# Reordering the projections and low-rank products at the head of an RWKV-7 time-mix stage

## The chip, the cores and the metric

The kernel is one launch on one core of a Trainium2 chip (trn2). The metric is the device time in microseconds of that core, as a median over runs. TensorE does the matrix products (PE, with its weight loads as PEld), VectorE is DVE, ScalarE is ACT, GpSimd is POOL, and SyncE (SP) issues the loads of the weights.

## The reference, cut to what matters

The program is a stack of blocks over 256 tokens of width 1024: feed-forward, a first mixer, feed-forward, a "fox" mixer, feed-forward, the RWKV-7 time mix, feed-forward. The change touches only the head of the time mix:

```python
xx = _token_shift(h) - h
xr, xw, xk, xv, xa, xg = [h + xx * mu[i] for i in range(6)]
r = (xr @ w_r).astype(f32)
k = (xk @ w_k).astype(f32)
v = (xv @ w_v).astype(f32)
w = -jax.nn.softplus(-(w0 + jnp.tanh(xw @ w1) @ w2).astype(f32)) - 0.5
a = jax.nn.sigmoid((a0 + (xa @ a1) @ a2).astype(f32))
g = jax.nn.sigmoid(xg @ g1) @ g2
...
kk = heads(k * k_k.astype(f32))
kk = kk / jnp.maximum(jnp.sqrt(jnp.sum(kk * kk, axis=-1, keepdims=True)), 1e-12)
k = k * (1.0 + (a - 1.0) * k_a.astype(f32))
decay = jnp.exp(-jnp.exp(w))
```

The recurrence over time is then computed in four chunks of 64 tokens with products of scaled r, k, kk and a; for that the running sum of log decays within each chunk, and exponentials of it, are needed.

## The kernel before

**Weights.** All weights come as one stream of chunks of 1 MB (128 partitions x 2048 fp32), loaded by SP in the order of the plan into three raw buffers. RWKV_ORDER is that plan for this stage: two low-rank chunks (L0, L1), then the four k chunks RW(4) to RW(7), the four r chunks RW(0) to RW(3), RW(8), the third low-rank chunk L2, RW(9) to RW(11) (v), and the output weights. The chunks of this stage ahead of L2 are "plain": TensorE reads them in fp32 from the raw buffer, so SP may load chunk c only when chunk c-3 has been used.

**Inputs.** The inputs of the six uses (k, w, a, g, r, v) are mixed by DVE: `mix_variant(v)` writes eight tiles of 128x256 into one of two buffers, variant_x[v % 2]; VARIANTS gives the order, 1 (w), 4 (a), 5 (g), 2 (k), 0 (r), 3 (v). From the third on it waits until the use two before has read its buffer (`variant_used`). The tiles of the first variant come out mixed with the subtraction for the token shift, so at half the pace.

**TensorE.** In `rwkv_tensor` three `first` groups (products with w1, a1, g1) go ahead, then `second` products (w2, a2) in four groups b, where groups 2 and 3 wait for ACT's sigmoids of groups 0 and 1 (rw_sig) since they share four PSUM banks. Then `project` runs the four k chunks, the four r chunks and the four v chunks, each 16 products into bank 6 or 7 in turn, and each waits until the chunk two before it has been read out of its bank (bank_read). Between the k chunks stand `square_sums(b)`, one product each, that sum the squares of kk per head.

**ACT.** In `rwkv_scalar` it takes tanh, copies and sigmoids of the low-rank products, then copies each k chunk into kx, squares kk, and takes the roots of the sums, `root(b)`. It then copies the four r chunks into rr. Before each copy stands this wait, since rr until then holds (a-1)*k_a, which DVE needs for k:

```python
projected(eng, name)
eng.wait_ge(s("rw_kx"), 4)
read(nc.scalar.activation(rr[:, 2 * j:2 * j + 2, :], bank2(proj_bank(name)), ACT.Copy), name)
```

Three exponentials of the decay sums (rw_exp 1 to 3) stand before, and two after, the copies: the first after the first k chunk, the others after the four r copies.

**DVE.** In `rwkv_vector` the order is: variants 0 to 4, the running sums (`tensor_tensor_scan`, eight) and their subtraction from sw (rw_before 1), (a-1)*k_a into rr (eight), then for each k chunk kk = kx*k_k (two) and kx = (rr+1)*kx (one, rw_kx). `unit_kk(b)` (maximum, reciprocal, product, each waited for by DVE itself) divides kk by its length; the first stands after the third k chunk, the other three after variant 5. Then aa*kk, kk*sw (rw_before 2), rk = r*r_k*k (eight, after all four r chunks are read), and three products with the exponentials, after which the chunked recurrence begins.

Of the kernel before, what the change touches and what calls it, by code (L numbers as in the profile page):

```python
# [20 lines left out]
P = 128  # L21
# [26 lines left out]
def stream_plan(stages):  # L48
# [18 lines left out]
RWKV_ORDER = [("lora", 0, 0), ("lora", 0, 1)] + [("rw", 0, j) for j in (4, 5, 6, 7, 0, 1, 2, 3, 8)] + \  # L67
    [("lora", 0, 2)] + [("rw", 0, j) for j in (9, 10, 11)] + [("rw_o", 0, j) for j in range(4)]
# [118 lines left out]
def build(nc, stream, consts, vectors, x_in, rows, kept_x, out):  # L187
# [15 lines left out]
    with ctx:  # L203
# [2019 lines left out]
        VARIANTS = (1, 4, 5, 2, 0, 3)  # L2223
        FIRST_OF = {3: 4, 4: 0, 5: 8}
# [14 lines left out]
        def variant_used(eng, v):  # L2239

            if v < 3:
                eng.wait_ge(s("rw_first"), v + 1)
            else:
                eng.wait_ge(chunk_used, USE[CH[RW(FIRST_OF[v] + 3)]] + 1)

# [11 lines left out]
        def rwkv_scalar(eng, highs, st):  # L2257
# [4 lines left out]
            for b in range(4):  # L2262
                eng.wait_ge(S["turned"], 4 * n + b + 1)
                for k in (2 * b, 2 * b + 1):
                    nc.scalar.activation(ht[:, k, 1:257], psum[:, b, (k % 2) * 256:(k % 2) * 256 + 256], ACT.Copy,
                                         scale=V_AT(NORMS[n], k)).then_inc(S["h_high"], 1)
            eng.wait_ge(s("rw_first"), 2)
# [16 lines left out]
            def root(b):  # L2284

                eng.wait_ge(s("rw_sums"), b + 1)
                nc.scalar.activation(roots[:, 2 * b:2 * b + 2, :], bank2(b), ACT.Sqrt).then_inc(s("rw_root"), 1)


            for j in range(4):  # L2290
                name = RW(4 + j)
                highs.upto(CH[name] + 2)
                projected(eng, name)
                read(nc.scalar.activation(kx[:, 2 * j:2 * j + 2, :], bank2(proj_bank(name)), ACT.Copy), name)
                highs.upto(CH[name] + 3)
                if j == 0:
                    eng.wait_ge(s("rw_before"), 1)
                    nc.scalar.activation(sw, sw, ACT.Exp, scale=-DECAY).then_inc(s("rw_exp"), 1)
                eng.wait_ge(s("rw_kk"), 2 * j + 2)
                nc.scalar.activation(roots[:, 2 * j:2 * j + 2, :], kk[:, 2 * j:2 * j + 2, :], ACT.Square).then_inc(s("rw_sq"), 1)  # L2300
                if j >= 2:
                    root(j - 2)

            for j in range(4):
# [127 lines left out]
        def rwkv_vector(eng, st):  # L2432
# [27 lines left out]
            for v in range(1, 4):  # L2460
                mix_variant(v)
            eng.wait_ge(S["rw_lw"], 6)
            nc.vector.tensor_tensor(gm_lo, lw[:, 1, :], gm_hi.bitcast(F32), ALU.subtract).then_inc(s("rw_lwlo"), 1)
            nc.vector.tensor_tensor(gt_lo, lw[:, 2, :], gt_hi.bitcast(F32), ALU.subtract).then_inc(S["rw_lwlo"], 1)
            mix_variant(4)

            eng.wait_ge(s("rw_sig"), 16)
            for k in range(8):
                ins = nc.vector.tensor_tensor_scan(sums[:, k, :], const("restart", TOK), sw[:, k, :], 0.0, ALU.mult, ALU.add)
            steps(ins)  # L2470
            nc.vector.tensor_tensor(sw, sums, sw, ALU.subtract).then_inc(s("rw_before"), 1)

            for k in range(8):
# [797 lines left out]
```

## Time and profile before

| | |
|---|---|
| Median of 3 runs | 1256.83 us (1256.41 to 1257.21) |
| The profiled execution | 1255.95 us |
| Its span, first to last instruction | 1254.2 us |
| PE busy | 1231.6 us, 98% |
| DVE busy | 531.8 us, 42% |
| ACT busy | 611.1 us, 49% |
| POOL busy | 766.4 us, 61% |
| The head of the time mix, first product to the end of the last r chunk | 831.58 to 912.99 us |
| The four v chunks | 912.99 to 944.28 us |

The span is counted from the first instruction to the last; what lies around it makes the execution 1.75 us longer. The profiled execution is 0.88 us below the median. A product in plain fp32 shows as two records of TensorE in the trace, so a chunk of 16 products is 32 records. The duration of a record includes the time through the array, in which the next one already runs: the pace is read from start to start.

### The profile page before, as it was taken

How to read it: one execution, taken by the hardware profiler on the slowest of the kernel's cores; microseconds unless marked ns; L12 is line 12 of the kernel's file. 1: busy time of each engine (PE TensorE's matmuls, PEld its weight loads, DVE VectorE, ACT ScalarE, POOL GpSimd, SP SyncE). 2: the span in 40 equal slices, each digit the busy share in tenths (PEclk: the TensorE clock that was granted, in tenths of full speed). 3: DMA queues.
4: the chain of work that ended last, by engine and by line, in shares of the span. 5: the costliest groups of instructions: out<-in, count | busy, mean ns of one | idle time of the engine just before them, and what ended most of it. 6: DMA issues, size and time to landing. Idle time of an engine off the chain costs nothing.

```text
span 1254.2 us, 22959 instructions
## 1 busy us (share of the span) xinstructions
PE 1231.6 (98%) x9568; PEld 1078.5 (86%) x9568; DVE 531.8 (42%) x818; ACT 611.1 (49%) x795; POOL 766.4 (61%) x194
## 2 busy tenths in 40 slices
PE   8999999999999999999999999999998999999998
PEld 7888887888988888899998888867887998888887
DVE  4233234745343233342533222375868645332333
ACT  7455444445464444584655445444232455544442
POOL 3988870262378888675478888800034324788885
PEclk9999999999999999999999999999999999999999
DMA  7655554244345555644245555513442013555552
GB/s 294 218 179 192 201 182 140 93 169 147 123 164 203 177 194 201 209 154 166 68 168 202 201 181 189 199 71 135 149 169 83 4 38 104 187 202 184 197 194 74
DMA packets 30587, 200.79 MB, mean 160 GB/s; under 512 B 3376, under 2 KB 5296, under 8 KB 6832
## 3 DMA queue, kind: packets, MB, share of 16 engines
q1 hardware_dynamic: 27776, 195.43, 44.3%
q10 hardware_dynamic: 2736, 4.26, 1.0%
q8 instruction: 59, 0.97, 0.3%
q14 instruction: 16, 0.13, 0.0%
HBM read 197.58 MB, written 2.10 MB: 159 GB/s over the span
## 4 chain that ended last, share of the span: by engine, by line
PE 91%; DVE 4%; ACT 2%; issue 1%; POOL 1%; DMA 1%; SPq 0%; POOLq 0%; DVEq 0%
PE psum L340 25%; PE psum L342 13%; PE psum L331 10%; PE psum L333 10%; PE psum L332 10%; PE psum L973 8%; PE psum L986 3%; POOL wlo L3167 1%; PE psum L2818 1%; PE psum L2723 1%; PE psum L2834 1%; PE psum L328 1%; PE psum L586 1%; PE psum L330 1%; PE psum L329 1%
## 5 line engine op out<-in xcount | busy, mean ns | idle before, releaser
L3167 POOL TENSOR_TENSOR wlo<-raw,whi 128x2048 fp32r<-128x2048 f32 x158 | 726.9, 4606 | 377.9 <-ACT whi L301 360.5
L340 PE MATMUL psum<-f_both,whi 128*128 128x512 f32 x1408 | 492.1, 393 | 1.4 <-DVE wlo L686 1.4
L301 ACT ACTIVATE whi<-raw 128x2048 fp32r<-128x2048 f32 x157 | 300.6, 1915 | 234.2 <-PE psum L342 169.4
L342 PE MATMUL psum<-f_both,wlo 128*128 128x256 f32 x1408 | 394.6, 280 | 0.0
L340 PEld LDWEIGHTS psum<-f_both,whi 128*128 128x128 f32 x1408 | 264.4, 188 | 60.1 <-DVE wlo L686 2.0
L342 PEld LDWEIGHTS psum<-f_both,wlo 128*128 128x128 f32 x1408 | 264.8, 188 | 1.5
L331 PE MATMUL psum<-whi,ahi 128*128 128x512 f32 x352 | 137.6, 391 | 0.3 <-POOL wlo L3167 0.3
L333 PE MATMUL psum<-whi,alo 128*128 128x512 f32 x352 | 137.2, 390 | 0.0
L332 PE MATMUL psum<-wlo,ahi 128*128 128x512 f32 x352 | 137.1, 390 | 0.0
L896 DVE TENSOR_TENSOR psum<-psum,arena 128x512 f32<-128x512 f32 x43 | 30.1, 700 | 241.8 <-ACT arena L612 241.7
L331 PE MATMUL psum<-whi,hhi 128*128 128x256 f32 x368 | 106.7, 290 | 2.6 <-DVE hlo L2686 1.2
L912 DVE TENSOR_TENSOR alo<-arena,ahi 128x512 fp32r<-128x512 f32 x44 | 95.2, 2164 | 31.7 <-ACT ahi L845 31.7
L333 PE MATMUL psum<-whi,hlo 128*128 128x256 f32 x368 | 104.0, 283 | 0.0
L332 PE MATMUL psum<-wlo,hhi 128*128 128x256 f32 x368 | 103.6, 281 | 0.0
L903 DVE TENSOR_TENSOR psum<-psum,arena 128x512 f32<-128x512 f32 x44 | 30.8, 700 | 171.3 <-ACT arena L612 171.3
L973 PE MATMUL psum<-arena,raw 128*128 128x256 f32 x448 | 101.8, 383 | 0.2 <-issue 0.2
L973 PEld LDWEIGHTS psum<-arena,raw 128*128 128x128 f32 x448 | 83.9, 190 | 14.4 <-issue 3.5
L331 PEld LDWEIGHTS psum<-whi,ahi 128*128 128x128 f32 x352 | 66.1, 188 | 14.3 <-POOL wlo L3167 0.6
L333 PEld LDWEIGHTS psum<-whi,alo 128*128 128x128 f32 x352 | 66.1, 188 | 13.9
L332 PEld LDWEIGHTS psum<-wlo,ahi 128*128 128x128 f32 x352 | 66.1, 188 | 12.1
L331 PEld LDWEIGHTS psum<-whi,hhi 128*128 128x128 f32 x368 | 69.2, 188 | 5.2 <-issue 3.8
L332 PEld LDWEIGHTS psum<-wlo,hhi 128*128 128x128 f32 x368 | 69.7, 190 | 0.0
(399 smaller groups left out, 1426.4 us busy)
## 6 DMA issues: line engine op xcount, KB each, us to landing
raw<-stream SPq DMA_DIRECT2D x182, 1024.0 KB, 4.9
con<-consts SPq DMA_DIRECT2D x1, 1216.0 KB, 13.8
x<-x_in SPq DMA_DIRECT2D x1, 1024.0 KB, 5.1
raw<-stream SPq DMA_DIRECT2D x2, 512.0 KB, 6.9
kept_x<-x ACTq DMA_DIRECT2D x1, 1024.0 KB, 3.9
x<-kept_x ACTq DMA_DIRECT2D x1, 1024.0 KB, 4.7
out<-x SPq DMA_DIRECT2D x4, 256.0 KB, 2.0
arena<-gm_w_s ACTq DMA_DIRECT2D x1, 512.0 KB
```

What stands on the lines that cost most here:

```text
L301: nc.scalar.activation(whi[:, slot, :], raw[:, c % RAW, :], ACT.Copy).then_inc(high_made, 1)
L331: nc.tensor.matmul(out, h_hi, w_hi, start=start, stop=False, skip_group_check=skip)
L332: nc.tensor.matmul(out, h_hi, w_lo, start=False, stop=False, skip_group_check=skip)
L333: return nc.tensor.matmul(out, h_lo, w_hi, start=False, stop=stop, skip_group_check=skip)
L340: nc.tensor.matmul(psum[:, bank, :].rearrange("p (a n) -> p a n", a=2), whi[w], f_both[:, :, k, :], start=k == 0, stop=False, skip_group_c ...
L342: return nc.tensor.matmul(psum[:, bank, 0:TOK], wlo[w], f_hi[:, k, :], start=False, stop=k == KT - 1, skip_group_check=True)
L896: nc.vector.tensor_tensor(left, left, aside[:, 0, :, :], ALU.add).then_inc(s("ffn_sum"), 1)
L903: nc.vector.tensor_tensor(left, left, aside[:, 1, :, :], ALU.add).then_inc(s("ffn_sum"), 1)
L912: nc.vector.tensor_tensor(flat(alo), act[:, b, :], flat(ahi).bitcast(F32), ALU.subtract)\
L973: mm = nc.tensor.matmul(psum[:, bank, j * 256:(j + 1) * 256], raw[:, slot, k * 256 + j * P:k * 256 + j * P + P], h[:, k, :], start=k == 0, ...
L986: mm = nc.tensor.matmul(psum[:, bank, m * 256:m * 256 + n], h[:, k, m * P:m * P + P], raw[:, slot, k * 256:k * 256 + n], start=k == 0, sto ...
L3167: nc.gpsimd.tensor_tensor(part(wlo[:, slot, :]), part(raw[:, c % RAW, :]), part(whi[:, slot, :]).bitcast(F32), ALU.subtract)\
```

## The change

The k chunks go ahead of the low-rank products, in the stream, on TensorE and on ACT. The `second` products run in two pairs, with the first half of RW(0) between them and its second half behind them. `square_sums(0)` to `(2)` stay behind the k chunks, and `square_sums(3)` stands between the first two `first` groups. The variants are made in the order k, w, a, g, r, v. On DVE the products with k_k (j = 0 to 3) come after variant 1, then variants 2, 3 and 4, the four `unit_kk`, the small low parts, variant 5, then (a-1)*k_a, the four updates of kx, and only then the running sums. On ACT all the roots come ahead of tanh and the sigmoids; the first exponential moves behind the copy of RW(0), and the other two behind the copy of RW(1).

```diff
-RWKV_ORDER = [("lora", 0, 0), ("lora", 0, 1)] + [("rw", 0, j) for j in (4, 5, 6, 7, 0, 1, 2, 3, 8)] + \
-    [("lora", 0, 2)] + [("rw", 0, j) for j in (9, 10, 11)] + [("rw_o", 0, j) for j in range(4)]
+RWKV_ORDER = [("rw", 0, j) for j in (4, 5, 6, 7)] + [("lora", 0, 0), ("lora", 0, 1)] + \
+    [("rw", 0, j) for j in (0, 1, 2, 3, 8)] + [("lora", 0, 2)] + [("rw", 0, j) for j in (9, 10, 11)] + [("rw_o", 0, j) for j in range(4)]
...
-        VARIANTS = (1, 4, 5, 2, 0, 3)
-        FIRST_OF = {3: 4, 4: 0, 5: 8}
+        VARIANTS = (2, 1, 4, 5, 0, 3)
+        FIRST_OF = {0: 4, 4: 0, 5: 8}
...
-            if v < 3:
-                eng.wait_ge(s("rw_first"), v + 1)
+            if 1 <= v < 4:
+                eng.wait_ge(s("rw_first"), v)
             else:
                 eng.wait_ge(chunk_used, USE[CH[RW(FIRST_OF[v] + 3)]] + 1)
...
# ACT (rwkv_scalar): the k chunks and all roots now stand ahead of tanh
+            for j in range(4):
+                name = RW(4 + j)
+                projected(eng, name)
+                read(nc.scalar.activation(kx[:, 2 * j:2 * j + 2, :], bank2(proj_bank(name)), ACT.Copy), name)
+                eng.wait_ge(s("rw_kk"), 2 * j + 2)
+                nc.scalar.activation(roots[:, 2 * j:2 * j + 2, :], kk[:, 2 * j:2 * j + 2, :], ACT.Square).then_inc(s("rw_sq"), 1)
+                if j >= 2:
+                    root(j - 2)
+            for b in (2, 3):
+                root(b)
...
             for j in range(4):
                 name = RW(j)
                 highs.upto(CH[name] + 2)
                 projected(eng, name)
                 eng.wait_ge(s("rw_kx"), 4)
                 read(nc.scalar.activation(rr[:, 2 * j:2 * j + 2, :], bank2(proj_bank(name)), ACT.Copy), name)
-                if j < 2:
-                    root(j + 2)
-
-            eng.wait_ge(s("rw_before"), 2)
-            nc.scalar.activation(sw, sums, ACT.Exp, scale=DECAY).then_inc(s("rw_exp"), 1)
-            eng.wait_ge(s("rw_exp"), 2)
-            nc.scalar.activation(sums, sums, ACT.Exp, scale=-DECAY).then_inc(s("rw_exp"), 1)
+                if j == 0:
+                    eng.wait_ge(s("rw_before"), 1)
+                    nc.scalar.activation(sw, sw, ACT.Exp, scale=-DECAY).then_inc(s("rw_exp"), 1)
+                if j == 1:
+                    eng.wait_ge(s("rw_before"), 2)
+                    nc.scalar.activation(sw, sums, ACT.Exp, scale=DECAY).then_inc(s("rw_exp"), 1)
+                    eng.wait_ge(s("rw_exp"), 2)
+                    nc.scalar.activation(sums, sums, ACT.Exp, scale=-DECAY).then_inc(s("rw_exp"), 1)
...
# DVE (rwkv_vector), the new order
+            mix_variant(1)
             for j in range(4):
                 name = RW(4 + j)
                 eng.wait_ge(bank_read[proj_bank(name)], PROJ[name] // 2 + 1)
                 for k in (2 * j, 2 * j + 1):
                     nc.vector.tensor_scalar(kk[:, k, :], kx[:, k, :], V_AT("k_k", k), None, ALU.mult).then_inc(s("rw_kk"), 1)
+            for v in (2, 3, 4):
+                mix_variant(v)
+            for b in range(4):
+                unit_kk(b)
+            eng.wait_ge(S["rw_lw"], 6)
+            nc.vector.tensor_tensor(gm_lo, lw[:, 1, :], gm_hi.bitcast(F32), ALU.subtract).then_inc(s("rw_lwlo"), 1)
+            nc.vector.tensor_tensor(gt_lo, lw[:, 2, :], gt_hi.bitcast(F32), ALU.subtract).then_inc(S["rw_lwlo"], 1)
+            mix_variant(5)
+
+            eng.wait_ge(s("rw_sig"), 16)
+            for k in range(8):
+                ins = nc.vector.tensor_scalar(rr[:, k, :], aa[:, k, :], 1.0, V_AT("k_a", k), ALU.subtract, ALU.mult)
+            steps(ins)
+            for j in range(4):
                 k = slice(2 * j, 2 * j + 2)
                 nc.vector.scalar_tensor_tensor(out=kx[:, k, :], in0=rr[:, k, :], scalar=1.0, in1=kx[:, k, :],
                                                op0=ALU.add, op1=ALU.mult).then_inc(s("rw_kx"), 1)
-                if j == 2:
-                    unit_kk(0)
-            mix_variant(5)
-            for b in range(1, 4):
-                unit_kk(b)
+            for k in range(8):
+                ins = nc.vector.tensor_tensor_scan(sums[:, k, :], const("restart", TOK), sw[:, k, :], 0.0, ALU.mult, ALU.add)
+            steps(ins)
+            nc.vector.tensor_tensor(sw, sums, sw, ALU.subtract).then_inc(s("rw_before"), 1)
...
# TensorE (rwkv_tensor), the new order
+            for j in range(4):
+                project(eng, RW(4 + j), plain_columns, h=variant_x[0], wait=made(0) if j == 0 else None)
+                if j:
+                    square_sums(j - 1)
+            eng.wait_ge(s("rw_root"), 1)
+            first(1, 0, 0, L0, 0, P, 256).then_inc(s("rw_first"), 1)
+            square_sums(3)
+            first(2, 0, 1, L0, 0, P, 256).then_inc(s("rw_first"), 1)
+            eng.wait_ge(s("rw_root"), 2)
+            first(3, 1, 0, L0, P, P, 256).then_inc(chunk_used, 1)
+            first(3, 1, 1, L1, D, 32, 32).then_inc(s("rw_first"), 1)
             eng.wait_ge(s("rw_lw"), 2)
+            eng.wait_ge(s("rw_root"), 4)
...
+            second(0)
+            second(1)
+            eng.wait_ge(s("rw_mixed"), 40)
+            for part in range(2):
+                quarter(eng, RW(0), plain_columns, part, variant_x[0])
+            second(2)
+            second(3).then_inc(chunk_used, 1)
+            for part in (2, 3):
+                quarter(eng, RW(0), plain_columns, part, variant_x[0])
+
+            for j in range(1, 4):
+                project(eng, RW(j), plain_columns, h=variant_x[0])
```

## Rows read from the trace of the kernel before

**Rows 1.** The page: busy time of the engines, and granted clock by slice.

```profile
PE 1231.6 (98%) x9568; PEld 1078.5 (86%) x9568; DVE 531.8 (42%) x818; ACT 611.1 (49%) x795; POOL 766.4 (61%) x194
...
PEclk9999999999999999999999999999999999999999
```

**Rows 2.** What TensorE waited for, whole span: total us, times, longest.

```profile
PE psum L2818 <- DVE arena L2561: 3.4, 3, 2.0
...
PE psum L2738 <- ACT arena L2282: 1.3, 2, 1.0
```

**Rows 3.** Timeline of TensorE from the stage's first products: start, us, work.

```profile
831.58 1.46 PE L2723 MATMUL psum<-arena,raw 128*128 128x256 f32 x4 [0.33 <-DVE arena L2442]
...
837.48 11.26 PE L2723 MATMUL psum<-arena,raw 128*128 128x256 f32 x50 [0.15 <-DVE arena L2442]
848.67 2.00 PE L2738 MATMUL psum<-arena,raw 64*128 64x256 f32 x16
...
868.12 1.02 PE L2746 MATMUL psum<-arena,con 128*128 128x512 f32 x2
868.98 7.07 PE L973 MATMUL psum<-arena,raw 128*128 128x256 f32 x32
...
892.27 20.88 PE L973 MATMUL psum<-arena,raw 128*128 128x256 f32 x96
912.99 13.33 PE L986 MATMUL psum<-raw,arena 128*128 128x256 f32 x61
```

**Rows 4.** Busy time by stretch: head of the stage; the v chunks.

```profile
831.58:912.99 81.41, 79.05 (x360) 63.28 (x361) 59.03 (x100) 26.64 (x46) 0.00 (x0) 1.00 0.35 119
...
912.99:944.28 31.29, 31.29 (x161) 27.77 (x159) 20.90 (x22) 11.18 (x10) 12.96 (x4) 1.00 0.47 168
```

**Rows 5.** Timeline of DVE in the same stretch.

```profile
837.40 9.58 DVE L2442 SCALAR_TENSOR_TENSOR arena<-arena,vec 128x256 f32<-128x256 f32 x24
850.20 0.42 DVE L2463 TENSOR_TENSOR alo<-arena,ahi 128x256 fp32r<-128x256 f32 x1 [3.22 <-ACT ahi L2275]
...
856.03 4.77 DVE L2469 TENSOR_TENSOR_SCAN arena<-con,arena 128x256 f32<-128x256 f32 x8 [1.90 <-ACT arena L2282]
860.83 2.29 DVE L2471 TENSOR_TENSOR arena<-arena 128x2048 f32<-128x2048 f32 x1
863.04 2.19 DVE L2474 TENSOR_SCALAR arena<-arena,vec 128x256 f32<-128x256 f32 x8
865.26 0.62 DVE L2490 TENSOR_SCALAR arena<-arena,vec 128x256 f32<-128x256 f32 x2
865.91 0.69 DVE L2493 SCALAR_TENSOR_TENSOR arena<-arena 128x512 f32<-128x512 f32 x1
...
888.97 0.42 DVE L2481 TENSOR_SCALAR arena<-arena 128x512 f32<-128x512 f32 x1
...
893.54 0.43 DVE L2481 TENSOR_SCALAR arena<-arena 128x512 f32<-128x512 f32 x1
...
914.09 6.58 DVE L2509 SCALAR_TENSOR_TENSOR arena<-arena,vec 128x256 f32<-128x256 f32 x8 [4.32 <-ACT arena L2309]
```

**Rows 6.** Timeline of ACT in the same stretch.

```profile
850.08 0.45 ACT L2281 ACTIVATE arena<-psum,vec 128x256 f32<-128x256 f32 x1
...
851.15 0.48 ACT L2282 ACTIVATE arena<-psum,vec 128x256 f32<-128x256 f32 x1
...
863.32 1.91 ACT L2298 ACTIVATE arena<-arena 128x2048 f32<-128x2048 f32 x1
...
868.32 0.60 ACT L2294 ACTIVATE arena<-psum 128x512 f32<-128x512 f32 x1 [1.78 <-PE psum L973]
...
911.09 1.91 ACT L301 ACTIVATE whi<-raw 128x2048 fp32r<-128x2048 f32 x1 [4.21 <-DMA raw<-stream]
```

**Rows 7.** Timeline of TensorE at the start of the program.

```profile
1.31 4.63 PE L348 MATMUL psum<-arena 128*128 128x256 f32 x10 [1.31 <-DVE arena L3218]
```

**Rows 8.** DMA issues in the stretch 800 to 990 us: size, median us to landing.

```profile
raw<-stream SPq DMA_DIRECT2D x19, 1024.0 KB, 4.9
```

More of the change, by code:

```diff
@@ L2266, in rwkv_scalar, with root @@
                                          scale=V_AT(NORMS[n], k)).then_inc(S["h_high"], 1)
+            def root(b):
+                eng.wait_ge(s("rw_sums"), b + 1)
+                nc.scalar.activation(roots[:, 2 * b:2 * b + 2, :], bank2(b), ACT.Sqrt).then_inc(s("rw_root"), 1)
+            for j in range(4):
[8 more added lines that the diff above has]
+                root(b)
             eng.wait_ge(s("rw_first"), 2)
@@ L2282, in rwkv_scalar @@
                 nc.scalar.activation(aa[:, k, :], bank2(4 + b)[:, k % 2, :], ACT.Sigmoid, bias=V_AT("a0", k)).then_inc(s("rw_sig"), 1)
[L2284 to L2302, printed above, removed]
             for j in range(4):
@@ L2458, in mix_variant @@
                     mix_tile(v, k)
[L2460 to L2473, printed above, removed]
-                ins = nc.vector.tensor_scalar(rr[:, k, :], aa[:, k, :], 1.0, V_AT("k_a", k), ALU.subtract, ALU.mult)
-            steps(ins)
             def unit_kk(b):
@@ L2726, in first, with square_sums, made, second @@
                 return mm
-            first(0, 0, 0, L0, 0, P, 256).then_inc(s("rw_first"), 1)
-            first(1, 0, 1, L0, 0, P, 256).then_inc(s("rw_first"), 1)
-            first(2, 1, 0, L0, P, P, 256).then_inc(chunk_used, 1)
-            first(2, 1, 1, L1, D, 32, 32).then_inc(s("rw_first"), 1)
+            def square_sums(b):
+                eng.wait_ge(s("rw_sq"), b + 1)
+                nc.tensor.matmul(psum[:, b, :], const("same64"), roots[:, 2 * b:2 * b + 2, :], start=True, stop=True)\
+                    .then_inc(s("rw_sums"), 1)
+            def made(v):
+                return lambda k: eng.wait_ge(s("rw_mixed"), 8 * v + k + 1)
+            for j in range(4):
[9 more added lines that the diff above has]
+            first(3, 1, 1, L1, D, 32, 32).then_inc(s("rw_first"), 1)
             eng.wait_ge(s("rw_lw"), 2)
-            for b in range(4):
+            eng.wait_ge(s("rw_root"), 4)
+            def second(b):
                 if b >= 2:
@@ L2741, in rwkv_tensor @@
                             mm.then_inc(s("rw_second"), 1)
-            mm.then_inc(chunk_used, 1)
-            def square_sums(b):
-                eng.wait_ge(s("rw_sq"), b + 1)
-                nc.tensor.matmul(psum[:, b, :], const("same64"), roots[:, 2 * b:2 * b + 2, :], start=True, stop=True)\
-                    .then_inc(s("rw_sums"), 1)
-            def made(v):
-                return lambda k: eng.wait_ge(s("rw_mixed"), 8 * v + k + 1)
-            for j in range(4):
-                project(eng, RW(4 + j), plain_columns, h=variant_x[1], wait=made(3) if j == 0 else None)
-                if j == 0:
-                    eng.wait_ge(s("rw_sig"), 16)
-                if j:
-                    square_sums(j - 1)
-            for j in range(4):
-                project(eng, RW(j), plain_columns, h=variant_x[0], wait=made(4) if j == 0 else None)
-                if j == 0:
-                    square_sums(3)
+                return mm
+            second(0)
[9 more added lines that the diff above has]
+                project(eng, RW(j), plain_columns, h=variant_x[0])
             def bonus_sum(m, k):
```

1 line of the change is left out of this document (removed).

## The prediction

> **What bounds the kernel now.** I read the page first: TensorE is busy 98% of the span and its granted clock is full in every slice [rows 1]. So a microsecond taken out of TensorE's own queue is worth a microsecond, and one of waiting added to it costs one; DVE and ACT have room on average, which says nothing about one stage. Then the waits of TensorE. The longest single wait anywhere is 2.0 us; in the part that the change touches the `second` products wait 1.3 us for ACT's sigmoids [rows 2]. Then the timeline of the stage [rows 3]: the first product starts at 831.58, the eighth at 837.48, because DVE makes the first variant's tiles more slowly than TensorE uses them; after that the queue is full to the end of the r chunks at 912.99. From 854 on nothing waits at all. The stretch is 81.41 us with 79.05 busy [rows 4], so at most 2.4 us of open gaps, and a little of slowed pace, are there to be won. DVE was busy only 59.03 us of the same stretch; the reader is to see here that 22 us of DVE's time are idle, and to ask where in the new order they lie.
>
> **The prices.** From starts in [rows 3]: three chunks take 912.99 - 892.27 = 20.72 us, so a chunk takes 6.91 and half a chunk, or one `first` group (8 products), 3.45. A square sum takes 868.98 - 868.12 = 0.86. Two groups b of `second` take 2.0 (the row of 16 records), so one takes 1.0. On DVE [rows 5]: a variant is a third of 9.58, 3.19; one `unit_kk` is 893.54 - 888.97 = 4.57; the low parts are two of 0.42 that overlap a little, 0.7; (a-1)*k_a is 865.26 - 863.04 = 2.22; an update of kx is 0.69 alone, and since such instructions overlap slightly I take 2.6 for four; the scans are 860.83 - 856.03 = 4.80 and the subtraction 2.29; the two products with k_k take 0.65 to the next start. On ACT [rows 6]: a copy of a chunk starts 0.20 after TensorE's next start (868.32 against 868.12) and takes 0.60; a large exponential 1.91. From the end of an ACT instruction to TensorE's next product I take 0.05: the fourth sigmoid ended at 851.63, and the products that waited for it began within that.
>
> **TensorE in the new order.** The front is unchanged in pace: the first half of RW(4) is fed by the same slow tiles, so its eighth product starts at 837.48 again, and the 2.9 us lost there (5.90 less 7 products of 0.43) stay lost. Then 0.43 for that product, 3.45 for the second half, and RW(5), a sum, RW(6), a sum, RW(7): 22.45. That puts the end of RW(7) at 863.81, which I call S. Behind it, if nothing waits: square sum 2 (0.86), `first` 1 (3.45) to S+4.3, square sum 3 (0.86), `first` 2 (3.45) to S+8.6, `first` 3 in both parts (6.91) to S+15.5, `second` 0 and 1 (2.0), half of RW(0) (3.45), `second` 2 and 3 (2.0), the other half (3.45) to S+26.4, RW(1) to S+33.3, RW(2) and RW(3) to S+47.15. That would be 910.96, 2.0 us sooner than before, the whole of the gain that is on offer: the 1.3 us of waits for sigmoids and some slow pace around them. These waits do go: ACT started its first one 1.4 us after `second` did (850.08 against 848.67) and its fourth 1.07 later, 0.36 each [rows 3, 6]; the same from S+15.5 ends all eight at about S+20, and `second` 2 comes at S+21.
>
> **What is late instead: DVE.** Between variant 1 (made by about 840.7) and the read of RW(7), DVE now has only 2.6 us of products with k_k to do: it idles some 17 us there, in front of the work that was done alongside. From S its queue is: RW(7)'s copy ends at S+0.83, products with k_k to S+1.48, variant 2 to S+4.67, variant 3 to S+7.86, then a wait for `first` 2 at S+8.8 to free the buffer, variant 4 to S+12.0, four `unit_kk` (18.28) to S+30.3, low parts to S+31.0, variant 5 to S+34.2, (a-1)*k_a to S+36.4, kx to S+39.0, scans to S+43.8, subtraction to S+46.1.
>
> ACT may copy RW(0) only after kx is done, S+39.0. Queued behind that copy are all the others, and behind the copies TensorE: RW(2) needs RW(0)'s bank. The copy ends at S+39.6, RW(2) starts at S+39.7 instead of S+33.3: TensorE waits 6.35 us. In the kernel before the same wait was free, since the updates of kx lay inside the k chunks. Next, the copy of RW(1) stands behind the first exponential, and that behind the subtraction: S+46.1, plus 1.91, plus the copy 0.60, with handoffs S+48.7. RW(3) needs that bank. RW(2) would end at S+46.6, so RW(3) waits another 2.1 us and ends at S+55.6. Third: aa*kk and kk*sw (2.3 each, the price of the subtraction, which has their size) bring rw_before 2 at S+50.7, two exponentials end at S+54.6 and RW(2)'s copy at S+55.2. RW(8) needs it at S+55.6: met by 0.4 to 0.6 us. So RW(3) ends at 863.81 + 55.6 = 919.4, against 912.99: 6.4 us later.
>
> **The clock.** The wait of 6.35 us is three times the longest in the trace, and during the 2.0 us one the clock held (granted clock 1.00 throughout [rows 1, 2]). What TensorE does after a longer rest shows only at the start of the program: ten records of 128x256 take 4.63 us, 0.46 each [rows 7], against 0.216 in this stage, which is the pace of 1.2 GHz against that of 2.4 (the page's row of the clock, averaged over slices of 31 us, doesn't show it). I take that it falls, and that coming back costs what it cost there, ten records at twice the time, 2.3 us. The bounds are nothing, and all of RW(2) at the low level, 6.9 us. RW(2) then ends at S+48.9 where RW(3) could start at S+48.7 anyway, so only 0.2 of the 2.3 counts. The Trainium skill ("TensorE: Matmul & The Clock Gate", section "Why this matters for your kernels") says to leave no idle gaps between bursts since they bring the clock down to half; it speaks against this change, and the trace neither confirms nor denies it for a wait this long. By the page the sum is 6.6 us, without the fall it is 6.4.
>
> **What comes behind is carried along.** The v chunks take 31.29 us as before [rows 4]. ACT's L2 copy (1.91 [rows 6]) now stands right before RW(3)'s copy and its data are there: SP can issue L2 when RW(2) is used, S+46.6, or S+48.9 with the slow clock, and a chunk lands 4.9 us after issue [rows 8], by S+54, while ACT comes to it at S+55.2. RW(3)'s copy ends at S+57.7, RW(9) needs it at S+62.5. DVE's rk (6.58 [rows 5]) ends at S+64.6, the bonus products stand in RW(10), S+69.4. Three products of 2.3 bring DVE to S+71.5, and TensorE wants the scaled tensors at S+86.9. Loads: each r chunk waits for the chunk three before, L0 (used S+12.1), L1 (S+23), RW(0) (S+26.4), and has over 5 us more than its 4.9. ACT's table loads, whichever of them move, fall into its waits for TensorE. Moved streams of SP and POOL wait for nothing new before L2.
>
> **The sum.** + 8.45 us of waits - 2.0 us + 0.2 us of clock = + 6.6 us. On the profiled span of 1254.2 that is 1260.8; with the 1.75 us around it and 0.88 to the median, 1256.83 + 6.6 = 1263.4 us.
>
> **Rivals.** (a) The waits are covered and the order pays: not slower. Its place is DVE's queue between S+1.5 and S+46. The end of RW(3) follows the exponential one for one, so each us that this queue is shorter gives one back; it has to be 4 us shorter for the time to fall within 0.2% of before (2.5 us, about what a measurement can tell), and 8.5 shorter for the full gain, 1256.83 - 2.0 = 1254.8. Two `unit_kk` running inside the idle time would do that, but they stand in program order behind variant 4. With 6.6 us off it comes out at 1256.8. For it speaks only DVE's low total; against it every row of [rows 5]. (b) The clock falls and stays low for all of RW(2): it ends at S+53.5, RW(3) at S+60.4, 11.2 us later than before, 1268.0; values between belong here too. For it speaks that no row shows the return after a long wait in mid-program; against it, the start's ten records. (c) The gates are a bit off: DVE's handoffs pile up (about a dozen of 0.05 to 0.1) and give 1264.4, or the overlaps are better and give 1262.4. (d) The change doesn't do what it says, the sigmoid waits stay: 1.3 us in TensorE's queue before S+33.3, where TensorE waits for DVE anyway, so the time is the same 1263.4.
>
> **Chances and range.** My forecast with (c) and (d), 1262.3 to 1264.5: 0.74. Longer low clock (b), 1264.5 to 1268: 0.12. A part of the wait covered, 1259.3 to 1262.3: 0.06. Rival (a), within 0.2%: 0.06, and beyond it, faster, 0.02. The range 1261.3 to 1266.0 holds the first, half of (b) and some of the partial one. Faster 0.02, same 0.06, slower 0.92.
>
> **What would show it.** In the timeline of TensorE: a gap of about 6.3 us before RW(2), put down to ACT's copy into rr, and about 0 to 2 us before RW(3); RW(2) taking 9.2 us (clock fell) or 6.9. The k phase ends at 863.8. On DVE: some 17 us idle before variant 2, and then none until kk*sw but the one us before variant 4. No wait of `second` for sigmoids. The v chunks start at 919.5 and last 31.3. Wrong if the kx updates are done before 897, if the gap is there but the later stages give it back, or if RW(8) waits as well.

## The result: 6.7 us slower

The changed kernel takes 1263.46 us (median of 5 runs, 1263.16 to 1263.79) against 1256.80 for the kernel before (5 runs, 1256.41 to 1257.21). The ratio is 1.0053, its 95% interval 1.0039 to 1.0068: slower, by 6.66 us. The forecast was 1263.4.

The page of the changed kernel, the lines that answer to [rows 1]:

```profile
span 1261.6 us, 22958 instructions
...
PE 1235.5 (98%) x9568; PEld 1081.6 (86%) x9568; DVE 530.7 (42%) x818; ACT 608.2 (48%) x793; POOL 767.1 (61%) x194
...
PEclk9999999999999999999999999999899999999999
```

The same number of products runs on TensorE, and its busy share is 98% in both: a page of shares doesn't show what happened. One digit of the clock's row does, an 8 among nines in slice 29. The waits of TensorE name the place (total us, times, longest), against [rows 2], where the same line is missing:

```profile
PE psum L973 <- ACT arena L2306: 5.8, 1, 5.8
```

L2306 is ACT's copy of an r chunk into rr. The timeline of TensorE, the rows that answer to [rows 3] (L2716 is `first`, L2723 a square sum, L2750 `second`, L973 a k or r chunk, L986 a v chunk):

```profile
832.19 1.46 PE L973 MATMUL psum<-arena,raw 128*128 128x256 f32 x4 [0.33 <-DVE arena L2440]
...
838.09 11.06 PE L973 MATMUL psum<-arena,raw 128*128 128x256 f32 x50 [0.16 <-DVE arena L2440]
...
864.51 1.02 PE L2723 MATMUL psum<-arena,con 128*128 128x512 f32 x2
...
880.25 2.00 PE L2750 MATMUL psum<-arena,raw 64*128 64x256 f32 x16
882.18 3.72 PE L973 MATMUL psum<-arena,raw 128*128 128x256 f32 x16
885.83 2.00 PE L2750 MATMUL psum<-arena,raw 64*128 64x256 f32 x16
887.76 10.63 PE L973 MATMUL psum<-arena,raw 128*128 128x256 f32 x48
904.20 16.21 PE L973 MATMUL psum<-arena,raw 128*128 128x256 f32 x64 [5.81 <-ACT arena L2306]
920.25 13.98 PE L986 MATMUL psum<-raw,arena 128*128 128x256 f32 x64
```

The last k chunk ends at 864.51, which is S. The groups of `second` wait for nothing any more: that part of the change works. Then there is a hole ahead of RW(2), and RW(2) with RW(3), which are 64 records, take 920.25 - 904.20 = 16.05 us, where 64 records of this kind took 13.8 before [rows 3]. The head of the stage, from the first product to the end of the r chunks, takes 88.06 us where it took 81.41 [rows 4]: 6.65 more. The rest of the 7.4 us between the two spans is 0.61 ahead of the stage, where nothing was changed, and 0.14 behind it.

Busy time by stretch for the changed kernel shows the slow part (after each stretch its length, then the busy time of PE, PEld, DVE, ACT and POOL with the number of instructions, then the granted clock, the DMA share and GB/s):

```profile
904.20:905.00 0.80, 0.80 (x2) 0.71 (x3) 0.80 (x2) 0.80 (x1) 0.00 (x0) 0.50 0.00 0
...
907.00:908.00 1.00, 1.00 (x4) 0.82 (x3) 1.00 (x2) 0.00 (x0) 0.00 (x0) 0.50 0.00 0
908.00:909.00 1.00, 1.00 (x4) 0.80 (x4) 0.97 (x2) 0.00 (x0) 0.00 (x0) 0.71 0.00 0
909.00:910.00 1.00, 1.00 (x6) 0.87 (x6) 1.00 (x1) 0.00 (x0) 0.00 (x0) 1.00 0.00 0
```

After the wait of 5.81 us TensorE has the clock at 0.50 (1.2 GHz) for over four microseconds, and is back at 1.00 (2.4 GHz) in the stretch from 909. The Trainium skill's advice against gaps between bursts ("TensorE: Matmul & The Clock Gate", section "Why this matters for your kernels") agrees with this trace; shorter waits than the page warns of were followed by a fall too, down to 2.01 us (last section).

DVE, the rows that answer to [rows 5]:

```profile
857.58 0.61 DVE L2471 TENSOR_SCALAR arena<-arena,vec 128x256 f32<-128x256 f32 x2 [7.15 <-ACT arena L2276]
865.34 0.62 DVE L2471 TENSOR_SCALAR arena<-arena,vec 128x256 f32<-128x256 f32 x2 [7.15 <-ACT arena L2276]
865.87 6.42 DVE L2440 SCALAR_TENSOR_TENSOR arena<-arena,vec 128x256 f32<-128x256 f32 x16
873.34 3.26 DVE L2440 SCALAR_TENSOR_TENSOR arena<-arena,vec 128x256 f32<-128x256 f32 x8 [1.05 <-PE psum L2716]
...
900.86 2.50 DVE L2487 SCALAR_TENSOR_TENSOR arena<-arena 128x512 f32<-128x512 f32 x4
903.28 4.76 DVE L2490 TENSOR_TENSOR_SCAN arena<-con,arena 128x256 f32<-128x256 f32 x8
908.07 2.29 DVE L2492 TENSOR_TENSOR arena<-arena 128x2048 f32<-128x2048 f32 x1
```

DVE sits idle for 7.15 us ahead of each of the last two k chunks' products (22.2 us in all in the k phase, with 1.64 and 6.29 ahead of the first two), and from 865 on it is the engine that everyone waits for. The updates of kx end at 903.4 and the subtraction behind the scans at 910.4. ACT, against [rows 6], waits for just these two, with the copy of RW(0) and with the exponential (L2309), behind which stands the copy of RW(1):

```profile
903.45 0.60 ACT L2306 ACTIVATE arena<-psum 128x512 f32<-128x512 f32 x1 [13.39 <-DVE arena L2487]
...
910.40 1.92 ACT L2309 ACTIVATE arena<-arena 128x2048 f32<-128x2048 f32 x1 [5.05 <-DVE arena L2492]
912.22 0.57 ACT L2306 ACTIVATE arena<-psum 128x512 f32<-128x512 f32 x1
...
918.68 0.58 ACT L2306 ACTIVATE arena<-psum 128x512 f32<-128x512 f32 x1
```

The last of these rows is the copy of RW(2).

### The profile page after: what moved, and what is told of

Read it like the earlier page. It is cut to its first block, busy times and chain, and to the rows that moved or that the text cites. A ratio compares the mean times of both kernels' runs of the same rounds, so it can differ in the third digit from the quotient of the medians.

```text
span 1261.6 us, 22958 instructions
## 1 busy us (share of the span) xinstructions
PE 1235.5 (98%) x9568; PEld 1081.6 (86%) x9568; DVE 530.7 (42%) x818; ACT 608.2 (48%) x793; POOL 767.1 (61%) x194
## 4 chain that ended last, share of the span: by engine, by line
PE 90%; DVE 5%; ACT 2%; issue 1%; POOL 1%; DMA 1%; SPq 0%; POOLq 0%; DVEq 0%; ACTq 0%
PE psum L340 24%; PE psum L342 12%; PE psum L331 10%; PE psum L333 10%; PE psum L332 10%; PE psum L973 7%; PE psum L986 3%; PE psum L2823 1%; POOL wlo L3172 1%; DVE arena L2463 1%; PE psum L2839 1%; DVE arena L2440 1%; PE psum L328 1%; DMA raw<-stream 1%; PE psum L586 1%
## 5 line engine op out<-in xcount | busy, mean ns | idle before, releaser
L973 PE MATMUL psum<-arena,raw 128*128 128x256 f32 x448 | 106.2, 391 | 7.3 <-ACT arena L2306 5.8
L973 PEld LDWEIGHTS psum<-arena,raw 128*128 128x128 f32 x448 | 84.4, 193 | 24.9 <-issue 9.7
```

The lines of the kernel that those rows point to most:

```text
L973: mm = nc.tensor.matmul(psum[:, bank, j * 256:(j + 1) * 256], raw[:, slot, k * 256 + j * P:k * 256 + j * P + P], h[:, k, :], start=k == 0, ...
```

## The experiments

In all of them the measure beside the time is the head of the stage, from the first k or low-rank product to the start of the v chunks, in each kernel's own profiled execution. The ratios are to runs of the kernel before that were taken beside each experiment; the medians of these lie between 1256.05 and 1256.82 us, so differences between rows of the table are read from the head first.

| kernel | median us | ratio to before (95%) | head, us |
|---|---|---|---|
| before | 1256.8 | | 81.41 |
| changed | 1263.46 | 1.0053 (1.0039 to 1.0068) | 88.06 |
| one_unit | 1258.12 | 1.0014 (1.0005 to 1.0023) | 83.15 |
| two_units | 1254.81 | 0.9988 (0.9979 to 0.9997) | 79.84 |
| kx_first | 1265.49 | 1.0073 (1.0059 to 1.0087) | 89.38 |
| exps_late | 1264.58 | 1.0065 (1.0051 to 1.0078) | 88.43 |
| kx_first_exps_late | 1254.89 | 0.9988 (0.9979 to 0.9998) | 79.84 |
| exps_late_idle | 1261.48 | 1.0036 (1.0022 to 1.0050) | 85.89 |
| after_idle | 1262.77 | 1.0048 (1.0034 to 1.0062) | 87.75 |
| two_units_unsplit | 1256.58 | 0.9999 (0.9990 to 1.0008) | 81.32 |
| unsplit | 1263.91 | 1.0055 (1.0040 to 1.0070) | 88.48 |
| before_split | 1260.01 | 1.0024 (1.0015 to 1.0034) | 85.25 |
| before_split_no_wait | 1258.63 | 1.0018 (1.0009 to 1.0028) | 84.17 |
| two_units_paired | 1251.28 | 0.9959 (0.9945 to 0.9972) | 76.95 |

### one_unit and two_units: shorten DVE's queue in two doses

```diff
# one_unit (DVE)
                     nc.vector.tensor_scalar(kk[:, k, :], kx[:, k, :], V_AT("k_k", k), None, ALU.mult).then_inc(s("rw_kk"), 1)
+                if j == 2:
+                    unit_kk(0)
...
-            for b in range(4):
+            for b in range(1, 4):
                 unit_kk(b)
```

```diff
# two_units (DVE, then ACT)
+                if j in (1, 2):
+                    unit_kk(j - 1)
...
-            for b in range(4):
+            for b in range(2, 4):
                 unit_kk(b)
...
-                if j >= 2:
-                    root(j - 2)
-            for b in (2, 3):
-                root(b)
+                if j:
+                    root(j - 1)
+            root(3)
```

> The changed kernel with one of the four normalisations of kk (unit_kk(0), 4.57 us of DVE) moved back into DVE's idle time among the k chunks. Theory A (DVE's queue after the last k chunk sets the end of the r chunks through ACT's copies, one us for one us): RW(2) may start 35.1 us after S (S is the end of the last k chunk; it was 39.7), TensorE is there at 33.7, so a wait of 1.4 us, short enough for the clock to hold; the copy of RW(1) frees its bank at S+43.8, RW(2) ends at S+42.0, a second wait of 1.7; the r chunks end at S+50.7 against S+55.7. Time 1258.4. Theory B (the low clock after the long wait is the main loss, the waits as such are small): 2.2 us back, 1261.2. Theory C (the new order of the stream or of TensorE's products costs the time): no change, 1263.5.

> The changed kernel with two normalisations (9.14 us) in DVE's idle time among the k chunks, and ACT's roots issued one chunk sooner so that they can be. Theory A: both waits vanish (RW(2) free at S+30.6, TensorE there at S+33.7; RW(3) free at S+39.2, TensorE there at S+40.6; RW(8) free at S+45.7, TensorE there at S+47.5); the r chunks end at S+47.5, 8.2 us sooner than in the changed kernel: 1255.3, 1.5 us below the kernel before. Theory B: 1261.2. Theory C: 1263.5.

Measured: 1258.12 and 1254.81. In one_unit the timeline of TensorE has two short waits where there was one long one:

```profile
899.40 7.14 PE L973 MATMUL psum<-arena,raw 128*128 128x256 f32 x32 [1.24 <-ACT arena L2306]
...
908.14 7.14 PE L973 MATMUL psum<-arena,raw 128*128 128x256 f32 x32 [1.59 <-ACT arena L2306]
```

RW(2) and RW(3) both run at the full pace, 7.14 us with the tail of the last record. In two_units the same part is one row without a wait:

```profile
887.67 24.44 PE L973 MATMUL psum<-arena,raw 128*128 128x256 f32 x112
911.95 13.98 PE L986 MATMUL psum<-raw,arena 128*128 128x256 f32 x64
```

The first dose of 4.57 us gives back 4.91 us of the head. The part above 4.57 is the clock's: against the changed kernel with the clock held up (after_idle, below, 87.75 us) it is 4.60. The second dose gives 3.31, when nothing is left to win. Theory A holds in both, B (1261.2) and C (1263.5) fall.

### kx_first, exps_late and both: which of the two waits counts

```diff
# kx_first (DVE)
-            for b in range(4):
+            for b in range(3):
                 unit_kk(b)
...
-            mix_variant(5)
-
             eng.wait_ge(s("rw_sig"), 16)
...
                                                op0=ALU.add, op1=ALU.mult).then_inc(s("rw_kx"), 1)
+            unit_kk(3)
+            mix_variant(5)
```

```diff
# exps_late (ACT)
                 read(nc.scalar.activation(rr[:, 2 * j:2 * j + 2, :], bank2(proj_bank(name)), ACT.Copy), name)
-                if j == 0:
-                    eng.wait_ge(s("rw_before"), 1)
-                    nc.scalar.activation(sw, sw, ACT.Exp, scale=-DECAY).then_inc(s("rw_exp"), 1)
-                if j == 1:
-                    eng.wait_ge(s("rw_before"), 2)
...
+
+            eng.wait_ge(s("rw_before"), 1)
+            nc.scalar.activation(sw, sw, ACT.Exp, scale=-DECAY).then_inc(s("rw_exp"), 1)
+            eng.wait_ge(s("rw_before"), 2)
+            nc.scalar.activation(sw, sums, ACT.Exp, scale=DECAY).then_inc(s("rw_exp"), 1)
+            eng.wait_ge(s("rw_exp"), 2)
+            nc.scalar.activation(sums, sums, ACT.Exp, scale=-DECAY).then_inc(s("rw_exp"), 1)
```

kx_first_exps_late has both edits. (In the kernel before, one exponential stood ahead of the copies of the r chunks and two behind them.)

> The changed kernel with (a-1)*k_a and the updates of kx moved ahead of unit_kk(3) and variant 5 on DVE; the scans stay where they were. It takes away the wait before RW(2) alone. Theory A, as refined: the end is set by the first exponential, which follows the scans, and ACT's copy of RW(1) behind it: the wait moves from before RW(2) to before RW(3) (7.7 us there, free at S+48.3), the clock falls there, where its 2.2 us are no longer hidden by the exponential: the r chunks end at S+57.4, 1.7 us later than in the changed kernel, 1265.2. Rival D (the wait on the kx updates is the cost): 6.0 us back and the clock's 2.2, 1255.3 to 1257.5.

> The changed kernel with ACT's three exponentials behind all four copies of the r chunks, as they partly were before. It takes away the wait on the exponential before RW(3) and leaves that before RW(2). Theory A: RW(2) starts at S+39.7 as before and takes 9.1 us at the low clock, RW(3) follows, which is what happened with the exponential in place: 1263.5, no change. Rival E (the exponential's 1.9 us and its wait in front of the copy count in full): 1261.4.

> The edits of kx_first and of exps_late together, each of which alone made the changed kernel slower or left it (1265.5, 1264.6). Theory A: they take away the two waits of which each hid the other: RW(2) free at S+31.7, RW(3) never waits for an exponential: the r chunks end at S+47.5, the head takes 79.8 us, 1255.0, as in two_units, though DVE does its four normalisations after S. Rival (what counts is DVE's idle time among the k chunks, so that only work moved into it helps): 1263 or more.

Measured: 1265.49, 1264.58, and 1254.89 together. With the wait ahead of RW(2) gone, the timeline of kx_first shows it ahead of RW(3), longer, and the clock's loss is in RW(3), 8.80 us where 7.14 is the pace:

```profile
887.56 17.53 PE L973 MATMUL psum<-arena,raw 128*128 128x256 f32 x80
912.73 8.80 PE L973 MATMUL psum<-arena,raw 128*128 128x256 f32 x32 [7.64 <-ACT arena L2306]
921.37 13.98 PE L986 MATMUL psum<-raw,arena 128*128 128x256 f32 x64
```

Its ACT shows why: RW(0)'s copy is 7.7 us sooner, counted from the first product, and the one of RW(1) still stands behind the exponential.

```profile
895.51 0.60 ACT L2306 ACTIVATE arena<-psum 128x512 f32<-128x512 f32 x1 [5.64 <-DVE arena L2485]
...
910.19 1.91 ACT L2309 ACTIVATE arena<-arena 128x2048 f32<-128x2048 f32 x1 [12.78 <-DVE arena L2493]
912.01 0.58 ACT L2306 ACTIVATE arena<-psum 128x512 f32<-128x512 f32 x1
```

In exps_late the wait ahead of RW(2) is the same 5.81 us:

```profile
904.08 16.58 PE L973 MATMUL psum<-arena,raw 128*128 128x256 f32 x64 [5.81 <-ACT arena L2306]
```

The head is nearly as long as before the edit (88.43 against 88.06): the clock stays low a little longer, and the 64 records take 16.42 us instead of 16.05. The median is 1.1 us above that of the changed kernel, where no change was expected (its runs go from 1263.42 to 1265.11). In the profiled executions the spans differ by 0.7 us, of which 0.37 lie in the head and 0.45 behind the v chunks, with 0.12 less ahead of the stage; why the low clock lasts longer stays open. Each edit alone wins nothing, and both together win 8.2 us of the head, to the same 79.84 us as two_units by another way: two waits in series, of which each hid the other, and both are DVE's lateness passed on by ACT. Moving work into DVE's idle time is one cure, and not the only one.

### exps_late_idle and after_idle: the clock's share

```diff
             for j in range(1, 4):
+                if j == 2:
+                    idle_constants(13, 0)
                 project(eng, RW(j), plain_columns, h=variant_x[0])
```

The idle products go into a bank whose content has been read; they are added to exps_late and to the changed kernel.

> The kernel of exps_late with 13 idle products (26 records, 5.6 us) of constants into a free PSUM bank, put between RW(1) and RW(2), where TensorE otherwise waits 5.8 us. Their results are used by nothing. RW(2) can start no sooner; what changes is only what TensorE does in the wait. Theory A with the clock's share: the clock holds, RW(2) takes 6.9 instead of 9.1 to 9.6 us, nothing stands behind it, the head of the stage takes 85.8 us instead of 88.4: 1261.2 to 1261.9 (1264.6 without the idle products). Rival (the slow pace of RW(2) comes from something else than the rest before it): no change, 1264.6.

> The changed kernel with the 13 idle products between RW(1) and RW(2), exponentials where the change put them. Theory A with the clock's share: the clock holds, RW(2) ends at S+46.6, but RW(3) is free only at S+48.3, so of the 2.2 us only 0.5 come back, and up to 0.3 more if the second, short stretch of low clock at the start of the chunked recurrence is gone too: 1262.8. Rival (the clock's 2.2 us count in full in the changed kernel): 1261.2.

Measured: 1261.48 and 1262.77. RW(2) starts no sooner; the timeline of exps_late_idle:

```profile
897.96 5.78 PE L375 MATMUL psum<-con 128*128 128x256 f32 x26
903.93 14.05 PE L973 MATMUL psum<-arena,raw 128*128 128x256 f32 x64 [0.19 <-ACT arena L2306]
```

The two r chunks take 14.05 us with the tail, 2.5 less than in exps_late, and the head 2.5 less. So the pace of RW(2) came from the rest ahead of it, and not from its operands. In after_idle the chunk is as fast, but a wait of 1.60 us opens behind it:

```profile
903.64 7.14 PE L973 MATMUL psum<-arena,raw 128*128 128x256 f32 x32 [0.21 <-ACT arena L2306]
912.38 7.14 PE L973 MATMUL psum<-arena,raw 128*128 128x256 f32 x32 [1.60 <-ACT arena L2306]
```

The head wins 0.31 us, the median 0.7. In the changed kernel the low clock is nearly hidden by the exponential, as the sum of the prediction had it.

### two_units_unsplit, unsplit, and two of before: what the split is worth

```diff
# two_units_unsplit and unsplit
             second(1)
+            second(2)
+            second(3).then_inc(chunk_used, 1)
             eng.wait_ge(s("rw_mixed"), 40)
-            for part in range(2):
-                quarter(eng, RW(0), plain_columns, part, variant_x[0])
-            second(2)
-            second(3).then_inc(chunk_used, 1)
-            for part in (2, 3):
+            for part in range(4):
                 quarter(eng, RW(0), plain_columns, part, variant_x[0])
```

```diff
# before_split: the kernel before, and this alone
                 if b >= 2:
                     eng.wait_ge(s("rw_sig"), 4 * (b - 1))
+                if b == 2:
+                    eng.wait_ge(s("rw_mixed"), 32)
+                    for part in range(2):
+                        quarter(eng, RW(4), plain_columns, part, variant_x[1])
...
-                project(eng, RW(4 + j), plain_columns, h=variant_x[1], wait=made(3) if j == 0 else None)
                 if j == 0:
+                    for part in (2, 3):
+                        quarter(eng, RW(4), plain_columns, part, variant_x[1])
                     eng.wait_ge(s("rw_sig"), 16)
+                else:
+                    project(eng, RW(4 + j), plain_columns, h=variant_x[1])
```

> The kernel of two_units, with the four groups of second products in a row again ahead of RW(0), as in the kernel before. It prices the split alone, where TensorE's queue is the bound. The waits for ACT's sigmoids (1.3 us) and the slower pace of lone groups come back: 5.5 us for the four against 3.9: 1256.3 to 1256.5, about the kernel before; ACT's sigmoids end sooner by some 2 us, which nothing needs. Rival (the 1.7 us gained by two_units come from elsewhere, the order of the square sums or the chunks): 1254.8.

> The changed kernel with the four groups of second products in a row ahead of RW(0), and nothing else. Theory A: TensorE reaches RW(2) some 1.6 to 1.9 us later, at about S+35.5, but may start it only at S+39.7 in either case, so the split is worth nothing here: 1263.5 (1263.1 to 1264.0). A shorter wait (4.2 us) may leave the clock up, which is hidden by the exponential but for 0.5 us. Rival (the split works in the changed kernel as in two_units, and the rest costs more): 1265.2.

> The kernel before, with the split alone: second groups 0 and 1, the first half of RW(4), groups 2 and 3, the second half of RW(4). Low-rank products still go ahead of the k chunks. From the rows of before: RW(4) ends 1.7 us sooner (859.5 for 861.2), but the last sigmoids come 2.3 us later (858.3), and with them the scans, (a-1)*k_a and the first kk, whose square TensorE needs at 866.4 and gets at 868.8: a wait of 2.4 us ahead of the first square sum, so RW(6) starts 0.7 us later than before: 1257.2. Rival (the wait for the sigmoids was the loss and its removal is kept): 1255.1.

Measured: 1256.58, 1263.91 and 1260.01. Where TensorE's queue is the bound (two_units) the split is worth 1.5 us of the head: without it the waits for the sigmoids are back, 1.01 and 0.32 us. In the changed kernel it is worth 0.4, and not because it spares these waits. Without it TensorE waits 4.34 us for ACT instead of 5.81 and starts RW(2) at the same S+39.7, but the two chunks take 16.46 us instead of 16.05. The rows of two_units_unsplit, then of unsplit:

```profile
883.60 1.14 PE L2751 MATMUL psum<-arena,raw 64*128 64x256 f32 x8 [1.01 <-ACT arena L2298]
```

```profile
903.78 16.63 PE L973 MATMUL psum<-arena,raw 128*128 128x256 f32 x64 [4.34 <-ACT arena L2306]
```

before_split is a miss: I expected 0.4 us slower and got 3.2. The timeline of TensorE:

```profile
848.78 2.00 PE L2742 MATMUL psum<-arena,raw 64*128 64x256 f32 x16
851.78 3.72 PE L973 MATMUL psum<-arena,raw 128*128 128x256 f32 x16 [1.00 <-ACT arena L2282]
...
870.27 1.13 PE L2750 MATMUL psum<-arena,con 128*128 128x512 f32 x2 [2.28 <-ACT arena L2300]
871.24 8.76 PE L973 MATMUL psum<-arena,raw 128*128 128x256 f32 x32
```

Two things are to be seen. TensorE still waits 1.00 us for a sigmoid (L2282), now ahead of the half chunk: I had put the half behind that wait and not ahead of it. And behind the wait of 2.28 us for the square, which was expected, RW(6) takes 8.76 us instead of 7.07: the granted clock is 1.00 to 871.20 and 0.50 from 872.20 to 875.00. So it was run again with the wait in its place:

```diff
# before_split_no_wait, against before_split
-                if b >= 2:
-                    eng.wait_ge(s("rw_sig"), 4 * (b - 1))
                 if b == 2:
                     eng.wait_ge(s("rw_mixed"), 32)
                     for part in range(2):
                         quarter(eng, RW(4), plain_columns, part, variant_x[1])
+                if b >= 2:
+                    eng.wait_ge(s("rw_sig"), 4 * (b - 1))
```

> The kernel of before_split had an error of placement: the wait for the first four sigmoids stood ahead of the first half of RW(4), so TensorE still waited 1.0 us there. Here it stands behind that half, as in the changed kernel. From the trace of before_split: the second pair of groups comes 1.4 us sooner and waits for nothing, the last sigmoid ends at 858.3, the scans start at 858.4, the square that TensorE wants at 866.4 is there at 868.9. Theory A: a wait of 2.5 us ahead of the first square sum, behind which the clock falls (1.7 us): RW(6) starts 0.9 us later than in the kernel before and ends 2.6 us later: 1259.4. If the clock holds, 1257.7. Rival (with the wait placed rightly the split pays in the old order as it does in two_units): 1255.3.

Measured: 1258.63, the head 84.17 us, 2.76 longer than in the kernel before. TensorE and then the clock around the first square sum:

```profile
851.16 3.72 PE L973 MATMUL psum<-arena,raw 128*128 128x256 f32 x16
854.81 2.00 PE L2742 MATMUL psum<-arena,raw 64*128 64x256 f32 x16
856.74 10.63 PE L973 MATMUL psum<-arena,raw 128*128 128x256 f32 x48
869.64 1.87 PE L2750 MATMUL psum<-arena,con 128*128 128x512 f32 x2 [2.28 <-ACT arena L2300]
```

```profile
870.00:872.00 2.00, 2.00 (x4) 0.93 (x3) 1.31 (x3) 0.70 (x2) 0.00 (x0) 0.50 0.71 299
```

No wait for sigmoids is left, and the kernel is slower than before by 0.18%. In the old order the sigmoids are on DVE's path to the first square: the scans, (a-1)*k_a and the first kk stand behind the last of them, so a split that makes them 2.5 us later makes TensorE wait for the square, and the clock falls behind that wait. Of the two orders that were run, the split pays only in the one with the k chunks ahead of it.

### two_units_paired: a version that beats both

```diff
-            for j in range(4):
-                project(eng, RW(4 + j), plain_columns, h=variant_x[0], wait=made(0) if j == 0 else None)
-                if j:
-                    square_sums(j - 1)
+            def paired_columns(slot, bank, h, wait):
+
+                for k in range(KT):
+                    wait(k)
+                    for j in range(2):
+                        mm = nc.tensor.matmul(bank2(bank)[:, j, :], raw[:, slot, k * 256 + j * P:k * 256 + j * P + P], h[:, k, :],
+                                              start=(k, j) == (0, 0), stop=k == KT - 1, skip_group_check=True)
+                return mm
+
+            project(eng, RW(4), paired_columns, h=variant_x[0], wait=made(0))
+            for j in range(1, 4):
+                project(eng, RW(4 + j), plain_columns, h=variant_x[0])
+                square_sums(j - 1)
```

> The kernel of two_units, with the 16 products of the first k chunk ordered by tile: both column halves of a tile one after the other, so that each of DVE's tiles (one in 0.855 us) feeds two products (0.86 us) instead of one. This is only possible since the k chunk, with 256 columns, now stands first. TensorE's 2.9 to 3.0 us lost to the slow tiles go, everything behind moves up, DVE included, whose queue is counted from the end of the k chunks: 1251.8. Rival (something else sets the pace there, or DVE's order becomes the bound): 1254.8.

Measured: 1251.28 us, 5.2 us below the kernel before and 12.2 below the changed one. The head is 76.95 us, and by the windows TensorE is busy in all of it:

```profile
831.65:908.60 76.95, 76.95 (x361) 63.77 (x362) 58.66 (x100) 28.49 (x47) 0.00 (x0) 1.00 0.36 125
```

The first chunk is one row of 32 records, 7.14 us, where the kernels without it wait six more times for a tile. It was 0.5 us better than expected; the head itself gave 2.89, the 2.9 to 3.0 of the sum. The rest isn't the edit's: in the profiled executions the first product starts 0.46 us sooner than in two_units, in a part of the program that is the same in both.

## Why the prediction was right, step by step

- **The front.** The end of RW(7) was put 32.23 us after the first product and came at 32.32 (864.51 - 832.19). The gaps of the first variant stayed, as said.
- **The gain.** TensorE's own queue was to be 2.0 us shorter. It is 1.6: two_units, without any wait for ACT, has a head of 79.84 against 81.41. The waits for sigmoids went. What was mis-sized is the half chunk between the pairs of `second` (3.65 us, 885.83 - 882.18, where 3.45 was taken) and the `first` groups 2 and 3 (10.57, where 10.36 was). two_units_unsplit shows that nearly all of the gain is the split (1.5 us); the order of the k chunks by itself shortens TensorE's queue by nothing, but before_split_no_wait shows that the split needs it, and two_units_paired what more it makes possible.
- **DVE's queue.** Its idle time in the k phase was given as some 17 us and is 22.2. That was a slip in the working, whose own figures (variant 1 made at 840.7, the copy of RW(7) read at 864.6, three pairs of products between) give 22; nothing in the sum hung on it. The prices, taken from rows of another order of the same instructions, held: the four `unit_kk`, the low parts, variant 5 and (a-1)*k_a each start within 0.1 us of where the queue had them, and kx is done at S+38.9, where S+39.0 was said. RW(2) was to start at S+39.7. It started at 904.20, S+39.69. The wait itself was 6.1 us from where TensorE's queue stood to that start, where 6.35 was said, since TensorE came 0.3 later. That this queue sets the time one for one is shown by one_unit: 4.60 us of the head for 4.57, clock aside.
- **The second gate.** RW(3) was to be free at S+48.7; ACT's copy ended at 912.79, S+48.3.
- **The third gate.** RW(8) was to be met by 0.4 to 0.6 us. The copy of RW(2) ended at 919.26, and RW(8) started at 920.25, 1.0 us later, without a wait.
- **The clock.** It fell, and cost 16.05 - 13.82 = 2.23 us, where 2.3 was taken from the start of the program [rows 7]. It was to count with 0.2, as the exponential held RW(3) anyway; it counts with 0.3 to 0.5. RW(3) could start when the copy ended, at 912.79, and started at about 913.34 (920.25 less a chunk of 6.91); after_idle gives back 0.3 of the head.
- **The sum.** Waits of 8.45 with 0.2 for the clock less 2.0 made 6.6. The parts as measured are 6.08 of wait and 2.23 of slow pace, less 1.66 of gain, 6.65. The gain was put 0.3 too high and the first wait 0.3 too long; that is one error and not two, since DVE fixed the start of RW(2), and TensorE was early for it either way. Likewise the second gate opened 0.4 us sooner, behind a clock that held RW(3) anyway. The luck is in the size of the clock's loss: the same fall cost 2.60 us in exps_late and 2.64 in unsplit, which would have made the total up to 0.4 us more.
- **What was said to be carried along** was: the v chunks take 31.29 us, from 920.25 to 951.54, and the stretch behind them is 0.14 us longer. The clock falls once more there, at the start of the chunked recurrence (last section), which the prediction didn't have.
- **Rival (a)**, that DVE's low share covers it, needed DVE's queue 4 us shorter for a time within 0.2% of before; one_unit, with 4.57 less, is at +0.14%. So the point was right too. The full gain was put at 1254.8, and two_units gave 1254.81.
- **Rivals (b) and (d)** fall: the clock is back at 1.00 from 909 on, within RW(2), and no `second` group waits.

## What to carry to other kernels

When a block of products is moved ahead of another on the engine that is the bound, list what the helpers do with each block's results, and where their idle time goes: here the k chunks left DVE idle for 22 us, and the work that had filled it came due afterwards. ACT copies results out of PSUM in program order, and here it passed on every wait that stood ahead of a copy, so a wait that was free in one order became the bound in another. Of two such waits in series, taking one away alone showed no gain (88.43 us) or a loss (89.38), and both together 8.2 us, so remove them together before either is judged. The pairing is worth a look wherever the first use of slowly made tiles has two halves.

## What the runs showed of the hardware

The clock falls after rests that are shorter than I had counted with. After waits of 7.64, 5.81 and 4.34 us of TensorE in the head of the stage the records start at 0.50. After the two waits of 2.28 us the clock falls too, but only once TensorE works again: in before_split it is 1.00 for the first 0.9 us. The work behind each of these waits lost 1.7 to 2.6 us. After waits of 1.24 to 1.60 us (one_unit, after_idle) the records were at 1.00.

At 2.0 us both are seen. Every kernel has a wait of 2.01 us at the start of the chunked recurrence. In the profiled executions of the kernel before, of one_unit, two_units and two_units_paired the clock stays at 1.00 behind it, in the others it falls; in the changed kernel, by stretch:

```profile
957.00:959.00 2.00, 2.00 (x43) 2.00 (x38) 1.93 (x4) 0.47 (x1) 1.25 (x1) 0.50 0.66 274
```

It needs no earlier fall (kx_first_exps_late and exps_late_idle have none in the head, and have this one). Whether it is a property of each kernel or changes from run to run, the timed runs don't say directly, since they have only a mean clock; but that mean varies within one kernel. The 71 timed runs of the kernel before that stand beside the experiments have means between 0.997 and 1.000. The 31 at 1.000 average 1256.21 us (1255.40 to 1257.75) and the 12 at 0.997 average 1257.09 (1256.60 to 1257.69). A lower mean clock goes with about 0.9 us of a scatter of 2.35, which is why the windows of the head were used beside the medians. What decides it is open.
